# Token-major, centred values in the recurrence; a later turn of the attention heads; waits and bonus steps moved

## The reference

```python
y = _wkv7_scan(rh, decay.reshape(B, T, H, N), kh, vh, kk, a.reshape(B, T, H, N))
mu = jnp.mean(y, -1, keepdims=True)
yc = y - mu
var = jnp.mean(yc * yc, -1, keepdims=True)
y = (yc * lax.rsqrt(var + GN_EPS)).reshape(B, T, C) * gn_g + gn_b
bonus = jnp.sum(rh * kh * r_k, -1, keepdims=True) * vh
y = y + bonus.reshape(B, T, C)
return (y * jax.nn.silu(g)) @ w_out
```

## Time and profile before

| | us |
|---|---|
| median of three runs | 2446.88 |
| lowest, highest | 2446.53, 2449.04 |
| the profiled execution, its own time | 2447.95 |
| its span in the trace | 2446.2 |
| TensorE busy | 2401.7 |
| VectorE busy | 1517.7 |
| ScalarE busy | 1187.3 |

### The profile page before, as it was taken

One profiled execution on the slowest core, in us unless ns is written; L12 is line 12 of the kernel. 1 busy time (PEld: TensorE's weight loads), 2 busy tenths in 40 slices (PEclk: granted clock), 3 DMA queues, 4 the chain that ended last, 5 costly groups with the idle time before them and its releaser, 6 DMA issues.

```text
span 2446.2 us, 49835 instructions
## 1 busy us (share of the span) xinstructions
PE 2401.7 (98%) x20771; PEld 2288.6 (94%) x20771; DVE 1517.7 (62%) x1848; ACT 1187.3 (49%) x1502; POOL 15.5 (1%) x31
## 2 busy tenths in 40 slices
PE   9999999989999999999999999999999999999998
PEld 9999999889999899999999999999999888999886
DVE  8577567657664445656789895565854444555445
ACT  5677353224454456664653346365544433444343
POOL 0000000000000000000000000000000000000000
PEclk9999999999999999999999999999999999999999
DMA  8355566314555555465456565655666655666664
GB/s 277 123 175 171 173 198 182 114 56 157 163 172 188 185 169 156 148 208 173 146 170 182 166 183 155 198 182 157 188 198 179 186 187 188 184 185 182 189 188 147
DMA packets 217225, 423.57 MB, mean 173 GB/s; under 512 B 17088, under 2 KB 19472, under 8 KB 216320
## 3 DMA queue, kind: packets, MB, share of 16 engines
q1 hardware_dynamic: 207520, 397.98, 52.9%
q0 software_dynamic: 2656, 12.17, 1.5%
q10 hardware_dynamic: 6864, 10.72, 1.4%
HBM read 412.43 MB, written 8.39 MB: 172 GB/s over the span
## 4 chain that ended last, share of the span: by engine, by line
PE 90%; DVE 6%; ACT 2%; issue 1%; ACTq 0%; DMA 0%; DVEq 0%; SPq 0%
PE ps L483 27%; PE ps L484 27%; PE ps L485 27%; PE ps L712 3%; DVE wlo L355 1%; ACT whi L351 1%; PE ps L629 1%; PE ps L615 1%; PE ps L720 1%; DVE act_lo L2056 0%; PE ps L919 0%; ACT regions L1451 0%; ACT L1451 0%; DVE regions L2083 0%; DVE regions L2080 0%
## 5 line engine op out<-in xcount | busy, mean ns | idle before, releaser
L355 DVE TENSOR_TENSOR wlo<-wraw,whi 128x1024 fp32r<-128x1024 f32 x752 | 917.6, 1224 | 840.3 <-ACT whi L351 839.2
L483 PE MATMUL ps<-act_hi,whi 128*128 128x256 f32 (+1 forms) x4736 | 1349.2, 285 | 14.2 <-DVE act_lo L2056 10.5
L484 PE MATMUL ps<-act_lo,whi 128*128 128x256 f32 (+1 forms) x4736 | 1333.0, 281 | 0.0
L485 PE MATMUL ps<-act_hi,wlo 128*128 128x256 f32 (+1 forms) x4736 | 1331.6, 281 | 0.0
L351 ACT ACTIVATE whi<-wraw 128x1024 fp32r<-128x1024 f32 x752 | 793.5, 1059 | 1070.3 <-PE ps L485 1046.1
L483 PEld LDWEIGHTS ps<-act_hi,whi 128*128 128x128 f32 x4736 | 891.1, 188 | 20.2 <-issue 14.8
L484 PEld LDWEIGHTS ps<-act_lo,whi 128*128 128x128 f32 x4736 | 894.1, 189 | 1.1
L485 PEld LDWEIGHTS ps<-act_hi,wlo 128*128 128x128 f32 x4736 | 891.2, 188 | 0.0
L484 PE MATMUL ps<-wlo,regions_r 128*128 128x512 f32 x512 | 203.0, 396 | 0.0
L485 PE MATMUL ps<-whi,regions_r 128*128 128x512 f32 x512 | 203.0, 396 | 0.0
L483 PE MATMUL ps<-whi,regions_r 128*128 128x512 f32 x512 | 203.0, 396 | 0.0
(11 more groups left out here) (331 smaller groups left out, 1470.5 us busy)
## 6 DMA issues: line engine op xcount, KB each, us to landing
wraw<-in_a_w_in SPq DMA_DIRECT2D x128, 512.0 KB, 3.8
wraw<-in_w_up SPq DMA_DIRECT2D x128, 512.0 KB, 3.8
wraw<-in_w_down SPq DMA_DIRECT2D x128, 512.0 KB, 4.3
wraw<-in_w_in SPq DMA_DIRECT2D x112, 512.0 KB, 3.7
wraw<-in_b_w_qg SPq DMA_DIRECT2D x64, 512.0 KB, 3.8
wraw<-in_a_w_out SPq DMA_DIRECT2D x32, 512.0 KB, 3.7
wraw<-in_w_k_shared SPq DMA_DIRECT2D x32, 512.0 KB, 4.3
wraw<-in_w_v_shared SPq DMA_DIRECT2D x32, 512.0 KB, 4.3
```

What stands on the lines that cost most here:

```text
L355: nc.vector.tensor_tensor(wlo[:, q % RING], wraw[:, q % RING], whi[:, q % RING].bitcast(F32), ALU.subtract).then_inc(lo_ready, 1)
L483: mm(o, hi_s, hi_m, start=first, stop=False, skip_group_check=True)
L484: mm(o, hi_s, lo_m, start=False, stop=False, skip_group_check=True)
L485: i = mm(o, lo_s, hi_m, start=False, stop=last, skip_group_check=True)
```

## The change

The v stage uses `wm_group`, so values come out token-major; ScalarE copies them to `V` in 8 operations per group, and the transposes are gone. The bonus sums are now one number per token and head (`rk_products`, 8 products with 2 columns per group), copied once to `rk_sums`. VectorE subtracts from `V` each head's mean over the values (`centre_values`, behind slabs 1, 4 and twice 16 of the g stage), and `gn_centre` is gone. The bonus is made token-major on ScalarE, one operation of 64 elements per head and chunk (`bonus`): centred value times sum plus mean times sum. Gain (`gn_rows`, loaded by GpSimd's queue at the very start and behind the gate) and bonus are applied token-major on VectorE in `gn_part2`; the offset and the gate come in one fused operation straight from PSUM (`z_full`). The bonus no longer passes through DRAM. Waits ahead of the recurrence move to the products that use their banks. The last chunk is normalised in parts of 4, 4 and 8 heads. Head turns move from slab 10 to slab 11.

```diff
+        bonus_of = lambda c: wk(3072, 1024) if c == 3 else TTs[:, c, :]
...
+                    pool.dma_start(gn_rows[n][side(p)].rearrange("t (i m) -> t i m", m=P),
+                                   ins["a_gn_g"][0:1].rearrange("o (i a m) -> o a i m", a=2, m=P)[:, p, 4 * n:4 * n + 4]
+                                   .broadcast_to([N, 4, P])).then_inc(S["gain_loaded"], 16)
+            load_gain(0)
...
-                pool.dma_start(bonus_at[part], bonus_dram[:, k0:k1, :]).then_inc(S[f"late_loaded{part}"], 16)
...
-            def vt(g):
-                def hook(q):
-                    if q == 1:
...
-                        for i in range(2):
-                            for c in range(4):
-                                m_ = nc.tensor.transpose(ps[:, 4 + i, c * P:(c + 1) * P],
-                                                         v_raw[:, i, c].rearrange("p a t -> p (a t)"), cs("ident"))
-                        m_.then_inc(S["vt_mm"], 1)
...
+            def rk_products(g):
+
+                pe.wait_ge(S["rk_ready"], g + 1)
+                if g == 0:
+                    pe.wait_ge(S["bcm_ready"], 4)
+                for c in range(4):
+                    for i in range(2):
+                        at = 2 * (KT // 2 * c + 2 * g + i)
+                        m_ = mm(ps[:, 6, at:at + 2], rk[g % 2][:, i, c].rearrange("p a t -> p (a t)"), cs("sel2"), start=True, stop=True)
+                m_.then_inc(S["rk_bc"], 1)
...
-                ws_group(G0["v"] + s, packed(2 * (s % 2)), T, ahi, alo, (lambda k: XS["v"] + k // 2 + 1) if s == 0 else None,
-                         vt(s - 1) if s else bc)
+                wm_group(G0["v"] + s, [bank(2 * (s % 2)), bank(2 * (s % 2) + 1)], ahi, alo,
...
                 if kind == "gather":
-                    pe.wait_ge(S["bvs_ready"], 4)
+                    pe.wait_ge(S["ab_ready"], 6)
                     pe.wait_ge(S["ab_packed"], 4)
...
-            pe.wait_ge(S["bvs_ready"], 4)
-            pe.wait_ge(S["silu_ready"], 4)
-            pe.wait_ge(S["lv_t"], 16)
+            pe.wait_ge(S["silu_ready"], 3)
...
-                    if n_ and it:
+                    if it == 0 and n_ == 0:
+                        pe.wait_ge(S["silu_ready"], 4)
+                    elif it == 0:
+                        pe.wait_ge(S["lv_t"], 16)
+                    elif n_:
...
-                pe.wait_ge(S["am_ready"], 6 * it + 6)
+                if it == 0:
+                    pe.wait_ge(S["v_centred"], 4)
                 for f in range(2):
+                    pe.wait_ge(S["am_ready"], 6 * it + 5 + f)
...
-                pe.wait_ge(S["yn_ready"], 4 + j2 // 4)
...
-            keep_warm(22, 0)
+            keep_warm(15, 0)
             for j2 in range(4):
                 turn_y(j2)
-            keep_warm(15, 0)
+            keep_warm(6, 0)
...
-                    if t == FIRST_HEAD + PER * h + 10:
+                    if t == FIRST_HEAD + PER * h + 11:
...
-                for i in range(2):
-                    st.do(a(as_tiles(v_raw[:, i]), in_tiles(four_t(bank(b0 + i))), ACT.Copy), sig["acc_act"] if i else None)
-                act.wait_ge(S["vt_mm"], s + 1)
                 if s == 0:
                     act.wait_ge(S["rnx_bc"], 4)
-                st.do(a(V[:, :, 2 * s:2 * s + 2, :], ps[:, 4:6, :].rearrange("p i (c m) -> p c i m", c=4), ACT.Copy),
-                      sig["v_ready"])
+                for c in range(4):
+                    for p in range(2):
+                        st.do(a(V[side(p), c, 2 * s:2 * s + 2, :],
+                                ps[side(c % 2), 2 * (s % 2) + c // 2, :].rearrange("t (i a m) -> t i a m", i=2, a=2)[:, :, p], ACT.Copy),
+                              sig["acc_act"] if c == 3 and p else None)
+
+            def bonus(c, h0, h1):
...
+                for h in range(h0, h1):
+                    i, f = divmod(h, 2)
+                    at = KT * c + h
+                    st.do(a(bonus_of(c)[:, h * N:(h + 1) * N], V[:, c, i, f * N:(f + 1) * N], ACT.Identity, scale=rk_sums[:, at:at + 1],
+                            bias=v_mean[:, at:at + 1]),
+                          sig["bonus_ready"] if h == HEADS // 2 - 1 else None)
...
+                if it:
+                    bonus(it - 1, 12, 16)
+                if it == 3:
+                    bonus(3, 0, 10)
...
+                    if it == 3 and f == 0:
+                        bonus(3, 10, 13)
...
-            gn_sqrt(3, 0, 8)
+                bonus(it, *((13, 16) if it == 3 else (0, 12)))
+            gn_sqrt(3, 0, 4)
+            gn_sqrt(4, 4, 8)
...
-            for j2 in range(8):
-                act.wait_ge(S["zt_mm"], j2 + 1)
-                if j2 >= 2:
-                    act.wait_ge(S["z_f"], j2 - 1)
-                for b in range(2):
-                    st.do(a(zt[j2 % 2][:, b * T:(b + 1) * T], ps[:, TURN_AT[j2], b * T:(b + 1) * T], ACT.Identity,
-                            bias=ve("gn_b", 2 * j2 + b), scale=ve("gn_g", 2 * j2 + b)), sig["z1_ready"] if b else None)
...
-                    if s and u == 3:
-                        bonus(s - 1)
+                    if u == 1:
+                        rk_terms(s)
+                    if (s, u) == (3, 6):
+                        dve.wait_ge(S["rk_bc"], 4)
+                        st.do(nc.vector.tensor_copy(rk_sums, ps[:, 6, 0:64]), sig["rk_taken"])
...
-            def gn_centre(i, h0=0, h1=16):
+            def gn_variance(i, n_=0, h0=0, h1=16):
 
                 dve.wait_ge(S["y_sb"], 2 * i + 2)
-                st.prev()
-                y, gsum = y_of(i)[:, h0:h1, :], gsums[:, h0:h1]
-                st.do(nc.vector.tensor_reduce(gsum, y, AX.X, ALU.add))
-                st.prev()
-                st.do(ts_(gsum, gsum, 1.0 / N, None, ALU.mult))
-                st.prev()
-                st.do(tt(y, y, gsum.unsqueeze(2).broadcast_to([P, h1 - h0, N]), ALU.subtract))
...
-                st.do(tt(y_of(i)[:, h0:h1, :], y_of(i)[:, h0:h1, :], gsums[:, h0:h1].unsqueeze(2).broadcast_to([P, h1 - h0, N]), ALU.mult),
-                      sig["yn_ready"])
+                y = y_of(i)[:, h0:h1, :]
+                st.do(tt(y, y, gsums[:, h0:h1].unsqueeze(2).broadcast_to([P, h1 - h0, N]), ALU.mult))
+                st.prev()
+                dve.wait_ge(S["gain_loaded"], 64)
+                for n in range(h0 // 8, (h1 + 7) // 8):
+                    at, end = max(h0, 8 * n), min(h1, 8 * n + 8)
+                    y_ = y_of(i)[:, at:end, :]
+                    st.do(tt(y_, y_, heads(gn_rows[n], 8)[:, at - 8 * n:end - 8 * n, :], ALU.mult))
+                dve.wait_ge(S["bonus_ready"], i + 1)
+                st.prev()
+                st.do(tt(y, y, heads(bonus_of(i))[:, h0:h1, :], ALU.add), sig["yn_ready"])
...
+                dve.wait_ge(S["acc_act"], s + 1)
+                v_ = V[:, :, 2 * s:2 * s + 2, :].rearrange("p c i (f n) -> p c (i f) n", n=N)
+                mean = v_mean.rearrange("p (c h) -> p c h", c=4)[:, :, 4 * s:4 * s + 4]
+                st.do(nc.vector.tensor_reduce(mean, v_, AX.X, ALU.add))
+                st.prev()
+                st.do(ts_(mean, mean, 1.0 / N, None, ALU.mult))
+                st.prev()
+                st.do(tt(v_, v_, mean.unsqueeze(3).broadcast_to([P, 4, 4, N]), ALU.subtract), sig["v_centred"])
...
-                    if (s, u) == (0, 4):
-                        bonus(3)
+                    for n in range(4):
+                        if 8 * s + u == (1, 4, 16, 16)[n]:
+                            centre_values(n)
...
                     gn_part2(it - 1)
-            gn_centre(3, 0, 8)
-            gn_variance(3, 0, 0, 8)
-            gn_part2(3, 0, 0, 8)
-            gn_centre(3, 8, 16)
+            gn_variance(3, 0, 0, 4)
+            gn_variance(3, 1, 4, 8)
+            gn_part2(3, 0, 0, 4)
+            gn_part2(3, 1, 4, 8)
...
-                dve.wait_ge(S["z1_ready"], j2 + 1)
-                st.do(tt(zt[j2 % 2], zt[j2 % 2], late(bonus_at, 2 * j2), ALU.add), sig["z_ready"])
-                st.prev()
-                st.do(tt(zt[2 + j2 % 2], zt[j2 % 2], late(gate_at, 2 * j2), ALU.mult), sig["z_f"])
+                    dve.wait_ge(S[f"late_loaded{2 * j2 // EARLY}"], 16)
+                dve.wait_ge(S["zt_mm"], j2 + 1)
+                for b in range(2):
+                    cols = slice(b * T, (b + 1) * T)
+                    st.do(stt(zt[j2 % 4][:, cols], ps[:, TURN_AT[j2], cols], ve("gn_b", 2 * j2 + b), late(gate_at, 2 * j2)[:, cols],
+                              ALU.add, ALU.mult), sig["z_f"] if b else None)
 
...
             z_full(1)
             z_lo(0)
-            gn_part2(3, 1, 8, 16)
-            for j2 in range(2, 8):
-                z_full(j2)
-                z_lo(j2 - 1)
-                if 4 <= j2 < 7:
-                    split_lo(dve, G0["wout"], j2)
+            gn_variance(3, 2, 8, 16)
+            z_lo(1)
+            z_full(2)
+            z_full(3)
+            z_lo(2)
```

(20 more changed lines are left out.)

115 lines of the change are left out of this document (51 added, 64 removed).

## The result

The changed kernel takes 2431.31 us (median of 4 runs, 2430.95 to 2432.74) against 2446.81 (2446.53 to 2449.04) on the same chip: ratio 0.9935, 95% interval 0.9922 to 0.9947. That is 15.5 us less; 18.6 were forecast. The profiled execution has a span of 2431.0 us.

The account below looks back on a forecast made before the run. TensorE, busy for 2401.7 of the 2446.2 us span, was taken as the bound. Terms of 20.6 us gained and 2.0 lost made 18.6, for a forecast median of 2428.3 us; range 2422.5 to 2437.0.

Parts of the forecast that it names:

- rival in which the clock drops stay: TensorE's clock drops stay or move, so 3.3 us less is gained: 2431.6 us; chance 0.22.
- Form, transposes, bonus sums: V stage: the new product form saves 1.5 us, 32 transposes gone save 3.5, bonus sums put at nothing.
- The gather: First g group's gather: TensorE's wait of 1.78 us goes, 1.8 us gained, between 0 and 1.8.
- Start of the recurrence: Recurrence's first products: of TensorE's 2.16 us wait some 0.35 is left, 1.8 us gained.
- Clock: Three TensorE clock drops, behind the gather and twice in the recurrence, go: 3.3 us gained, between 0 and 3.3.
- Bonus steps: ScalarE in the recurrence: 64 operations at 0.37 us each slightly delay the copies of turned keys, 0.5 us lost.
- rival of long steps: ScalarE's bonus steps take their full 0.59 us each, costing 9.7 us more: 2438.0 us; chance 0.05.
- U copy of the last step: Recurrence's last step: three bonus steps between the two U copies delay the second, 0.8 us lost on the path.
- From the recurrence to wout: Last Y copy to output projection: VectorE's new chain takes 7.8 us instead of 11.5, 3.7 us gained.
- Start of the kernel: Gain load of 256 KB beside the first inputs and weights: 0.7 us lost, between 0 and 2.
- The sign that I named: Kernel start: the prediction is wrong if the first matmul of all comes over 2 us later.
- Fetch gaps: Rival: TensorE's "issue" gaps in the recurrence also go, some 4 us: 2424.3 us; chance 0.07.

Follow-up runs that it names:

- e_before_gain: The kernel before with only two unused gain loads of 128 KB added at the very start on GpSimd's queue: 2449.61 us, ratio 1.0009.
- e_before_turns: The kernel before with only the head turns moved a slab later, from 10 to 11: 2440.82 us, ratio 0.9975.
- e_before_waits: The kernel before with only the recurrence's first waits moved to the products using their banks, and masks awaited by halves: 2444.77 us, ratio 0.9989.
- e_warm_start: The changed kernel with 40 instead of 28 unused matmuls ahead of the first real one: 2431.47 us.
- e_more_transposes: The changed kernel with 8 unused transposes ahead of each of the four groups of bonus sums: 2437.25 us, ratio 0.9960.
- e_late_bonus_y: The changed kernel with the first gain half loaded behind the v stage and three last-chunk bonus steps moved behind the Y copies: 2428.58 us.

## Why the prediction was right, and where it missed

Direction and size were right: 2431.3 lies in the range of 2422.5 to 2437.0, 3.0 us above the forecast. It also lies 0.3 from the 2431.6 of the rival in which the clock drops stay, and there only by chance: the clock is 1.00 in the recurrence, and what is missing was lost at the start. The time alone would have pointed to the wrong account.

- **Form, transposes, bonus sums: 5.0 forecast, 5.0 measured.** The stretches of the v stage gained 6.8, of which 1.8 is the gather's wait. Transposes put back cost 3.56 for the 3.5 of the working. The 1.4 that remain are form and bonus sums together, and no run tested them apart. (68.2 / 3 is 22.73, not the 22.75 of the working; the term stays 1.5.)
- **The gather: 1.8, as forecast.** VectorE's packing ended 0.6 us ahead of TensorE (0.8 by my count).
- **Start of the recurrence: 1.8 forecast, 1.1 measured.** The wait of 2.16 became 1.03, not 0.35. The 0.35 rested on some 1.7 us for the products that now go ahead of it, as between 483.50 and 485.23; but those ran at the lower clock. At the full one they fill 1.1 us.
- **Clock: 3.3 forecast, and the drops are gone in this profile.** For the one behind the masks (1.7) the mechanism is shown, in the profiles with and without the long wait; for the other two it is not. The size was off in three ways. The drop at 484 us also slowed the products ahead of L820, 0.8 us more than I counted. It and the one behind the gather are not in every profile of versions that share this code: in e_before_gain and e_before_turns, without either, the stretch from the gather to the second products took 124.9 us instead of 126.5. And the one behind the gather doesn't follow the length of the wait: it is there behind 1.78 (the kernel before) and 1.13 us (e_before_waits), and not behind 1.84 (e_before_gain) and 1.22 (e_before_turns). What a returned clock gives back can also go into a longer "issue" gap, as e_before_waits shows.
- **Last step: 0.6, as forecast** (2.04 to 1.43).
- **Bonus steps: 0.5 lost by forecast, right as an upper bound.** TensorE has no wait for the copies of turned keys in the profile. A step takes 0.34 us, 0.37 was estimated. By the page of the Trainium skill on VectorE's modes ("VectorE: DVE Perf Modes", section on the TRN2 errata) the estimate was 0.24; the trace doesn't agree with it. The rival of long steps had the mechanism right and its price too low: at twice the work it is 17.7 us, not 10, since 26 steps stand ahead of the last W copy, which TensorE alone awaits for 7.6 us, and since two of the three waits of over 3 us (3.63 and 7.62, not 3.50) are also followed by a stretch at the lower clock.
- **U copy of the last step: 0.8 lost by forecast, at most 0.3 in profiles.** I had counted the steps on the path, and TensorE's own gap covers them. Two profiles (e_warm_start and e_more_transposes) have a wait of 0.29 for that copy.
- **From the recurrence to wout: 3.7 forecast, 3.2 measured.** I priced what the change builds, and not the alternative: the split in 4 and 4, which I took as a help, costs 0.7 of it.
- **Head turns: 4.4 forecast, 4.7 in the profile of the edit alone, 5.1 from wout to the end in the changed kernel.**
- **Start of the kernel: 0.7 lost by forecast, some 4 measured. This is the step that failed.** It was worked as "256 KB at 266 to 278 GB/s is 1.0 us, not all of it ahead of the first slab", that is, as a share of a stream that is anyway full. What counts there is not the stream but the arrival of one chunk: the 256 KB of x that TensorE's first matmul needs landed 1.4 to 2.1 us later. Nor were the stretches of 266 and 278 GB/s full ones: those behind the first matmul here move 384 and 350 GB/s, and at that rate the 256 KB would be 0.7 us. And I had let the delay end with itself, though my own list of clock drops said what follows a long wait of TensorE: here 1.4 to 2.6 us of slow matmuls. The sign that I named, the first matmul over 2 us late, was just met in the first profile (2.02) and not in the second (1.37); the upper end of 2 us for the whole loss was too low.
- **Fetch gaps.** The "issue" gaps stayed (that they come from fetching instructions is shown by no run): 8.0 us in all after, 9.4 before, and 4.9 to 9.2 in the other profiles.

## What to carry to other kernels

Whatever is loaded at the very start can delay the one chunk that the first matmul waits for. What is needed only hundreds of microseconds later should be issued behind a wait that ends well after the start and well before the use. Price a wait of TensorE by its length and by the clock behind it, and read from several profiles how often that drop occurs. Splitting the serial chain into parts gained nothing here, because nothing downstream was ordered to start on the first part.

## What the runs showed of the hardware

- A load of 256 KB on GpSimd's queue, issued 0.5 us after SyncE's first load, put off SyncE's second chunk of x by 1.4 to 2.1 us, with pieces of 512 bytes and of 2 KB alike. In one profile without the load (e_late_bonus_y) that chunk was 0.75 us late all the same.
- The same wait ahead of the same code is followed by a drop of TensorE's clock in some profiles and not in others: after 2.16 us in the kernel before, with 1.00 in e_before_gain and e_before_turns. A drop also occurred at the start with a wait of only 1.91 us (e_before_turns, 0.50 in 12 to 14 us).
- "Issue" gaps of TensorE in the recurrence stay, but move. The recurrence took 67.7 to 69.7 us in five profiles of versions whose code in it is the changed kernel's, and 70.5 and 71.7 in two more. A difference of 3 us in one profile of this stretch is no evidence for an edit.
